# Loading one expert of the second layer after the first row fetches instead of before them

## The reference

```
combine = sum(one_hot(e_global, 32) * e_w)        # 2 experts per token
a = einsum('nd,edf->nef', t, w_g)                  # d = 1024, f = 256
u = einsum('nd,edf->nef', t, w_u)
y = einsum('nef,efd->nd', silu(a) * u * combine, w_d)
x = layernorm(alpha * x + gate * y) * gain + bias
```

## Time and profile before

| what | value |
|---|---|
| median of 3 runs | 974.54 us (974.33 to 977.64) |
| span of the profiled execution, first to last instruction | 968.9 us |
| own time of the profiled execution | not listed apart from its span |
| busy share: TensorE, VectorE, ScalarE, GpSimd | 85%, 35%, 15%, 18% |
| moved by DMA | 321.39 MB, mean 332 GB/s |
| mean granted TensorE clock | 0.958 of full speed |

### The profile page before, as it was taken

One profiled execution on the slowest core, in us unless ns is written; L12 is line 12 of the kernel. 1 busy time (PEld: TensorE's weight loads), 2 busy tenths in 40 slices (PEclk: granted clock), 3 DMA queues, 4 the chain that ended last, 5 costly groups with the idle time before them and its releaser, 6 DMA issues. The chain is left out here.

```text
span 968.9 us, 12777 instructions
## 1 busy us (share of the span) xinstructions
PE 821.1 (85%) x4895; PEld 419.4 (43%) x4895; DVE 339.3 (35%) x818; ACT 147.5 (15%) x339; POOL 176.8 (18%) x250
## 2 busy tenths in 40 slices
PE   3899999998898897998869788999599987777783
PEld 2555666665457433333323234546433333333331
DVE  3113554556587211111111137848611111101036
ACT  1122222223200111111101012001111110101013
POOL 2041212123122211122111100223212211111100
PEclk9999999999997999999999999999699999999998
DMA  9998493439339897999999979976899999999971
GB/s 333 365 371 305 140 386 112 167 135 342 145 105 387 353 412 290 420 420 418 419 418 419 418 304 356 381 264 230 353 387 418 417 419 418 419 419 420 419 297 65
DMA packets 91020, 321.39 MB, mean 332 GB/s; under 512 B 12686, under 2 KB 25710, under 8 KB 66872
## 3 DMA queue, kind: packets, MB, share of 16 engines
q1 hardware_dynamic: 74400, 289.41, 75.7%
q0 software_dynamic: 12704, 21.86, 6.3%
q10 hardware_dynamic: 3832, 8.99, 2.5%
HBM read 313.62 MB, written 28.90 MB: 354 GB/s over the span
## 5 line engine op out<-in xcount | busy, mean ns | idle before, releaser
L1067 PE MATMUL psum<-ring,arena 128*64 128x512 f32 x880 | 255.2, 629 | 39.1 <-DMA ring<-in_w_expert_up 28.4
L1067 PEld LDWEIGHTS psum<-ring,arena 128*64 128x64 f32 x880 | 84.8, 145 | 169.4 <-issue 166.0
L1089 PE MATMUL psum<-ring,arena 128*64 128x512 f32 x440 | 124.1, 598 | 20.2 <-DVE arena L1883 19.6
L1879 DVE TENSOR_TENSOR arena<-arena,psum 128x256 f32<-128x256 f32 x34 | 14.3, 421 | 283.6 <-ACT arena L1408 277.0
L1067 PE MATMUL psum<-h_hT,arena 128*64 128x512 f32 x208 | 93.1, 601 | 6.0 <-DMA ring<-in_w_expert_up 5.1
L937 PE MATMUL psum<-ring,h_hT 128*128 128x384 f32 x288 | 96.5, 488 | 0.0
L883 PE MATMUL psum<-ring,h_hT 128*128 128x512 f32 x160 | 69.3, 593 | 1.8 <-ACT h_hT L1489 1.5
L684 POOL DMA_INDIRECT y_scratch<-arena,sidx x32 | 33.6, 1048 | 203.9 <-DVE arena L1889 203.9
L937 PEld LDWEIGHTS psum<-ring,h_hT 128*128 128x128 f32 x288 | 53.6, 191 | 34.1
L1089 PEld LDWEIGHTS psum<-ring,arena 128*64 128x64 f32 x440 | 35.6, 136 | 71.2 <-issue 46.8
L1889 DVE COPY arena<-psum 128x512 f32<-128x512 f32 x32 | 22.1, 692 | 120.6 <-PE psum L1089 120.6
(11 more groups left out here) (230 smaller groups left out, 890.0 us busy)
## 6 DMA issues: line engine op xcount, KB each, us to landing
ring<-in_w_expert_down SPq DMA_DIRECT2D x52, 1024.0 KB, 20.6
ring<-in_w_expert_gate SPq DMA_DIRECT2D x50, 1024.0 KB, 19.0
ring<-in_w_expert_up SPq DMA_DIRECT2D x50, 1024.0 KB, 22.2
ring<-in_w_ada SPq DMA_DIRECT2D x24, 2048.0 KB, 15.0
h_hT<-in_w_expert_gate SPq DMA_DIRECT2D x12, 1024.0 KB, 20.4
h_hT<-in_w_expert_up SPq DMA_DIRECT2D x12, 1024.0 KB, 24.0
h_hT<-in_w_expert_down SPq DMA_DIRECT2D x12, 1024.0 KB, 26.5
ring<-in_w_qkv SPq DMA_DIRECT2D x9, 1024.0 KB, 12.5
```

The lines of the kernel that those rows point to most:

```text
L1067: last = pe.matmul(bank[b][64 * e:64 * e + 64, :].rearrange("p (g n) -> p g n", g=2), mem.GT[b][:, c, 64 * e:64 * e + 64], w, start=(c == ...
L1089: last = pe.matmul(bank[5 + half][64 * e:64 * e + 64, :], mem.actT[b][:, f, 64 * e:64 * e + 64], w[:, f, 512 * half:512 * half + 512], sta ...
L1879: V.tensor_tensor(mem.act[b], mem.sil[b], bank[b][:, FE:2 * FE], ALU.mult).then_inc(S["act"], 1)
```

## The change

In the preloads of layer 1, expert 1 comes ahead of expert 3, and SP waits for the first two row fetches before it issues expert 3. The wait for unit 11 of `w_ada` stays ahead of expert 3. No byte is added or left out, and no other engine's program changes.

```
                     sp.wait_ge(proj_ps, 12)
                     load_expert(1, 0)
+                    after_ada(1, 10)
+                    load_expert(1, 1)
+                    first_rows_fetched(1)
                     after_ada(1, 11)
                     load_expert(1, 3)
-                    after_ada(1, 10)
-                    load_expert(1, 1)
                     load_last_slot(1)
```

## The result

The changed kernel has a median of 979.24 us over 7 runs (975.41 to 985.56); the kernel before, in 7 runs beside it, 974.54 us. The ratio is 1.0056, with a 95% interval of 1.0036 to 1.0075. It is slower by 4.7 us by the two medians and by 5.5 us by the ratio (3.5 to 7.3), where +5.5 us was forecast. A second series of 12 runs gave 1.0028 (1.0015 to 1.0040), that is 2.7 us, so the size is better told as some 3 to 5.5 us.

A forecast was written before the change was run, and what follows sets the result against it. The prediction took layer 1's saturated weight stream to bound the kernel. Expert 3's bytes +7.5, earlier fetch landing -0.7 and filled hole -1.3 gave +5.5 us, 980.0 us from 974.54, range 977.1 to 981.8 us.

The forecast's parts named there:

- What bounds the end: Layer 1's unbroken weight stream at 418 to 420 GB/s sets the end, by its start and its bytes.
- First and third term: Expert 3's 3.146 MB join the stream, +7.5 us; the DMA dip behind expert 4 at 710 to 714 us fills, -1.3 us.
- Second term: At SP's wait, the second row fetch lands sooner on idle DMA engines: -0.7 us, bounds 0 and -3.1.
- an end of SP's wait more than 2 us earlier: At SP's wait for the row fetches: ending over 2 us earlier than before would show the prediction wrong.
- the 2.6 us given for it: First row fetch lands at 696.2 instead of 698.84 us, 2.6 us sooner, which only TensorE gets.
- the fetches' issue does not move: On GpSimd, the row fetches' issue stays put, since it waits for VectorE's table of rows, not for a transfer.
- The rival of the fast fetches, (a): Second fetch takes near 2.2 us on idle engines, hole gives 1.7: sum +2.7 us, 977.2 us; chance 0.27.
- Rival (b): TensorE sets the end, so the first fetch's 2.6 us gain passes through: 971.9 us; chance 0.04.
- Rival (c): Expert 3 lands too late for pair 1, after 717 us; over +7.1 us, 981.6 us; chance 0.04.
- Pairs 2 to 5 still have slack for this: In layer 1, these pairs can absorb weights from expert 4 on arriving 5 to 6 us later each.
- the prediction had said one pair: First pair waiting for a weight stands one pair earlier, or waits about 5 us longer.
- the idle window from 691 us on: Ahead of expert 3, DMA nearly idle between about 691 and 700 us, in place of 697 to 700.

The follow-up runs named there:

- order alone: Against the changed kernel: expert 1 still ahead of expert 3, but no wait for the row fetches before expert 3; 976.08 us, 1.0015.
- changed, at the fetch's issue: Against the changed kernel: SP goes on to experts 3 and 4 when the second row fetch is about to be issued, not when both landed; 974.83 us, 1.0007.
- before, no wait for expert 4: Against the kernel before: expert 4 of layer 1 loaded as soon as its slot is free, without waiting for the row fetches; 974.58 us, 1.0011.
- before, at the fetch's issue: Against the kernel before: order of experts kept, expert 4 issued when the second row fetch is about to be issued; 976.88 us, 1.0018.
- before, small matmuls: Against the kernel before: 26 small identity matmuls on TensorE in the gaps between layer 1's routing steps; 973.92 us, 0.9992.
- down matrix behind: Against the changed kernel: only expert 3's down matrix stays behind the wait for the fetches, its gate and up go ahead; 976.78 us, 1.0026.
- an eighth of expert 3: Against the changed kernel: only an eighth of each matrix of layer 1's expert 3 is loaded, wait and order kept; 972.57 us, 0.9985.
- changed, small matmuls: Against the changed kernel: 26 small identity matmuls on TensorE in the gaps between layer 1's routing steps; 976.89 us, 1.0029.
- changed, small matmuls, at the fetch's issue: Against the changed kernel: 26 identity matmuls in layer 1's routing gaps, and SP goes on when the second row fetch is about to be issued; 975.00 us, 1.0004.
- both experts behind: Against the changed kernel: expert 1 as well as expert 3 of layer 1 loaded behind the wait for the row fetches; 985.02 us, 1.0105.

## Why the prediction was right

**What bounds the end.** Right, and shown. In every trace TensorE waits for weights at pair 13 (0.4 to 3.6 us), and at pair 14 it waits again (1.2 to 2.9 us) or, in the second trace of the kernel before and in the third with small matmuls, begins within 0.2 us of their landing. The stretch behind pair 14's start keeps its 54.0 to 54.3 us. In the ten experiments with an edit the stretch from the fetch's issue to pair 14, less the 223.6 us of before, comes within 1 us of what the ratio of times gives. The traces give two earliest times for pair 14: SP's release plus 214 us (214.2 in the kernel with the order alone, 214.4 in the kernel before with the small matmuls), plus 7.5 us for each expert behind it; and pair 0's end (the loop's first issue) plus 203.3 to 203.9 us:

| kernel | release to pair 14 | pair 0's end to pair 14 |
|---|---|---|
| before (two traces) | 215.8, 215.3 | **203.3, 203.3** |
| changed (two traces) | **222.3, 222.1** | 211.0, 210.7 |
| changed, at the fetch's issue | **222.1** | 206.1 |
| before, no wait for expert 4 | 229.6 | **203.9** |
| before, at the fetch's issue | 224.0 | **203.4** |
| order alone | **214.2** | 204.1 |
| before, small matmuls | **214.4** | 204.1 |
| down matrix behind | **216.8** | 205.4 |
| an eighth of expert 3 | 216.5 | 205.3 |
| changed, small matmuls | **222.1** | 211.5 |
| changed, small matmuls, at the fetch's issue | **222.5** | 208.3 |
| both experts behind | **229.2** | 212.3 |

The later of the two decides (bold). This reproduces every start of pair 14 to 0.8 us except that of the kernel with an eighth of expert 3, which comes 1.4 us later than either gives. In the kernel before both lie close together, with pair 0 the later by the dip of the earlier trace rows. In the changed kernel only the release counts.

**First and third term, bytes and hole.** Forecast +7.5 - 1.3 = +6.2 us. Measured, release to pair 14: 222.2 - 215.5 = +6.7 us. Taking the bytes away took the loss away, and doubling them gave +7.0 us more. The two can be told apart by the kernel with the order alone, in which pair 0's end is not what decides (715.46 + 203.3 = 918.8 us, pair 14 begins at 919.51, and the windows show no hole): its 214.2 us are the stream without a hole. From there two experts cost 15.0 us, 7.5 each, as 3.146 MB at 418 GB/s do, and the hole of the kernel before is 215.5 - 214.2 = 1.3 us. One expert by itself reads 8.0, so each term is good to half a microsecond, and the sum is 0.5 us above the forecast.

**Second term, the earlier release.** Forecast -0.7 us, with bounds of 0 and -3.1. Measured from the fetch's issue to the release: 7.4 and 8.7 us before, 6.0 and 5.8 after, so -2.2 us on average (-1.4 by the first pair of traces, -2.9 by the second). This is the term that was mis-sized. The prediction had named an end of SP's wait more than 2 us earlier as a sign that it is wrong, and by the average this term passes it. There are two reasons. The nearest row for a landing in idle queues, the scatter's 4.6 us, was too long: the second fetch, for which SP waits, took 3.8 us, some 1.5 less than before instead of 0.7 less. And the one trace at hand had a quick fetch, 7.2 us against 8.4 in the second. The first fetch gained less than the 2.6 us given for it in the first pair of traces (5.7 against 7.2), since it did not find the engines idle: they were at 1.00 from 694 to 696 and at 0.75 from 696 to 698 us. On idle engines both fetches take 2.6 us (both experts behind the wait), which is the row that the prediction lacked. That the fetches' issue does not move holds as far as the traces can tell, 25.0 to 26.2 us behind expert 0's issue in both kernels.

**The sum** then is +6.7 - 2.2 = +4.5 us, beside +5.5 forecast, and beside +4.7 and +3.1 us in the two series of medians. That the first median, 979.24 us, came so close to the forecast of 980.0 is in part luck: the two errors of +0.5 and -1.5 us partly cancel, and the second series gave 977.64. The rival of the fast fetches, (a), had the right sign for its deviation: the fetches did land faster than forecast (3.8 us, where it took 2.2), while the hole was 1.3 us as forecast and not 1.7. Whether the loss is above or below 0.5% is not settled by the runs (1.0036 to 1.0075, 1.0015 to 1.0040). That it is a loss is.

**Rival (b), faster**, fell: pair 0 did end earlier counted from the fetch's issue (17.4 and 17.2 us against 19.9 and 20.6), and none of it came through. **Rival (c)** fell too: pair 1 began at 716.74 us without a wait.

**A step that was wrong.** "Pairs 2 to 5 still have slack for this": pair 3 waited 0.9 us (1.2 in the second trace) and pair 4 3.6. By TensorE's pace of 12.7 us it would have begun at 754.9 us, and it began at 759.56, when the up matrix of expert 9 landed. The long waits begin two pairs earlier than before, where the prediction had said one pair, without changing the end, which is fixed by the bytes. And the idle window from 691 us on did not show; the start-up gap between experts 0 and 1 (DMA share 0.16, 0.24 and 0.80 at 682 to 688 us, 3.6 us idle) took part of it, which the prediction had allowed only "a microsecond or two".

## What to carry to other kernels

In a kernel that ends in one saturated stream of transfers, count bytes on either side of the stream's start: a load moved behind it costs its whole transfer, here 7 us for 3.1 MB, and gets back only what the wait in front becomes shorter. Look for what opens the stream, and there may be two gates close together, here SP's wait and the first pair's end; filling idle DMA time ahead of the later gate brings nothing. Lay two traces on each other at an event ahead of the change before subtracting anything, since the spans alone gave 7 us for a change of 4.5.

## What the runs showed that I had not expected

- The same program's executions differ by up to 7 us (970.96 to 978.21 us in the 29 runs of the kernel before that ran beside the down matrix, the missing wait and the fetch's issue), and part of it is there ahead of the change: expert 0 of layer 1 was issued between 665.4 and 671.4 us in the traces, though nothing ahead of it differs between these kernels.
- The granted clock stood at 0.50, the 1.2 GHz level, from 692 to 696 us in the kernel with the small matmuls, while TensorE was busy 2.00 of 2.00 us in each window. Work in the gaps delayed the fall (0.50 was first reached in the window from 692 us, against 684 and 682 us in the two traces of the kernel before) and brought the full level back earlier, but did not prevent the fall. In the changed kernel the clock fell to 0.50 at 682 to 684 us though TensorE had been busy 2.00 of 2.00 us in every window from 674 us on.
- A row fetch's landing depends on what is still queued when it is issued, more than the first trace showed: 8.8 to 9.0 us for the first fetch of the four kernels in which the DMA engines stayed full up to 702 us or longer (order alone, down matrix behind, no wait, kernel before at the fetch's issue), 5.7 us for the first and 3.8 us for the second fetch of the changed kernel, and 2.6 us for both on idle engines.
